# Second-table rows scaled in place by ScalarE and summed as accumulating transposes

## The chip, the cores and the metric

The kernel runs on one core of one Trainium2 chip. The metric is the device time of one execution in microseconds (us). Engine names in the profile: PE is TensorE, PEld its weight loads, DVE VectorE, ACT ScalarE, POOL GpSimd, SP SyncE.

## The reference

The input is 256 tokens of width 2048. A first block (two layers: sliding-window attention beside a gated recurrence, then stick-breaking attention) and a second block (a state-space group beside gated attention) come first; their matrix work fills about the first 1540 us. The change touches only what follows, a layer of looked-up experts ("peer"):

```
q = (t @ wq)...; s1, s2 = scores of q against two sets of 128 keys     # per token, 8 heads
idx, sc = top 16 of the sums of the top 16 of s1 and of s2             # 8 x 16 = 128 picks a token
g = softmax(sc)
act = gelu(einsum('thkd,td->thk', u[idx], t))                          # first table, rows of 2048 floats
out = einsum('thk,thkd->td', g * act, v[idx])                          # second table
x = x + out;  result = rmsnorm(x) * lnf_w
```

Both tables have 16384 rows of 2048 fp32. All arithmetic is fp32.

## The kernel before

**Picks.** Tokens lie on the 128 partitions, in two groups m = 0, 1. A "row" n of 256 is one pick for each of 128 tokens: n = 128 m + pick. For each row POOL starts one indirect DMA that fetches 128 rows of 8 KB (1 MB) of the first table into UROW (4 buffers) and one for the second table into VROW (5 buffers; the last four rows go into UROW). The last 16 blocks of 128 experts are "dense": they are not gathered (a pick that points there is skipped by the bounds check) but computed for all tokens, with table pieces that SP loads into DROW, 32 halves of 512 KB per table.

**First table.** DVE multiplies UROW with the tokens and sums along the row (L2162), one instruction a row. After every four rows ACT takes GELU (L1334), and DVE multiplies with the gates (`coefficients`, L2070), which gives COEF. DVE does this for batch q of four rows after its product of row 4q+5 and waits there for the GELU.

**Second table.** Row v runs V_LAG = 8 rows behind. In `diagonals` ACT makes a diagonal matrix of the 128 coefficients of a row (L1321, 128x128, four buffers). PE multiplies it with the row in four fp32 matmuls of 512 columns (`mm`, the last loop; the helper's line in the trace is L2223), accumulating in banks 0 to 3 with tokens on partitions. That completes row v and frees VROW (semaphore `v_used`). Every eighth row in two stretches, and four near the end, DVE adds itself in one instruction (`ON_DVE`, L2092). After row 127 DVE adds the banks to XR (`add_outputs`, at row 136), and PE waits for that before row 128.

**Order on the queues.** Every engine's order is written out by hand. POOL goes through n = 4 to 263: it waits until DVE is done with row n-4 and starts the fetch of row n of the first table (L668), then waits until VROW is free of row n-13 and starts the fetch of row n-8 of the second table (L676). ACT does, for each q: wait for four products, GELU of batch q, then `diagonals(q - 1)` with its other work for those rows beside it. PE takes the second-table rows in order, and beside them (`beside_row`) the dense work: for rows 2 to 109 turning pieces of the first table (L2785) and their products (`dense_dots`, 256 columns), for rows 112 to 158 gate matrices from one-hots, for rows 161 to 226 `dense_values`, the dense part of the second table, in which m = 1 goes to banks 0 to 3 (those of the rows) and m = 0 to banks 4 to 7. DVE adds banks 4 to 7 at row 236 (`add_dense`).

**The end.** DVE adds what is left, the squares, the root and the scaling follow, and SP stores the result.

Of the kernel before, what the change touches and what calls it, by code (L numbers as in the profile page):

```python
# [26 lines left out]
P = 128  # L27
# [23 lines left out]
HT_STEPS = 8  # L51
BATCH = 4
N_PICKS = MT * PICKS
ADD_AT = PICKS + 8
ADD_DENSE_AT, SUM_AT, SCALE_AT = PICKS + 108, PICKS + 113, PICKS + 121
ON_DVE = tuple(v for v in range(60, 108) if v % 8 == 7) + tuple(v for v in range(160, N_PICKS - 8) if v % 8 == 7)\
    + (N_PICKS - 7, N_PICKS - 5, N_PICKS - 4, N_PICKS - 2)
LATE = N_PICKS - 4
SHARED = N_PICKS - 1
LAST_ORDER = (2, 3, 0, 1)  # L60
# [28 lines left out]
def rows_before(rows, v):  # L89

    return sum(r < v for r in rows)
# [147 lines left out]
def two_blocks(nc, a, out):  # L239
    ctx = ExitStack()  # L240
    with ctx:
# [25 lines left out]
        with ExitStack() as rounded:  # L267
# [40 lines left out]

        names = """
            const_in ln_first vec_in masks vec_t cols_set x_in out_done eps_set act_chain dve_chain pool_chain  # L310
            w_full0 w_full1 w_full2 w_full3 w_gate0 w_gate1 w_gate2 w_gate3 g_t r_of r_v r_c r_hi r_lo r_one wh_done wl_done ws_used tile_free half_left low_out
            n_rstd n_root n_sq n_sum n_x n_t n_xt n_h n_l r_diag r_row r_set t_scaled y_ready y_h y_l
            aq_ready qk_t qk_c
            a_score a_soft a_exp a_rcp a_pn a_pt a_ptc a_pv
# [5 lines left out]
            k_in k_t k_c q_s q_sc tk_idx tk_e tk_g ln_in  # L320
            u_row0 u_row1 u_row2 u_row3 v_row0 v_row1 v_row2 v_row3 v_row4
            u_dot p_gelu p_coef p_diag v_used v_on o_add
            tt_set d_row0 d_row1 d_t d_tc d_m d_act d_v g_in g_g g_mix
            """.split()
        s = {n: sem(n) for n in names}
# [72 lines left out]
        GATE_PARTS = g_bf[:, 2048:2816].rearrange("p (k t) -> p k t", k=3)  # L398
        I1T, I2T, IOTA_B = g_bf[:, 2816:3072], g_bf[:, 3072:3328], g_bf[:, 3328:3456]
        G_REST = BIG[:, 13, 768:1024]  # L400
        DONE = [BIG[:, 12:14, :].rearrange("p a b -> p (a b)"), BIG[:, 10:12, :].rearrange("p a b -> p (a b)")]

        def v_buffer(v):
# [38 lines left out]
        @block.sync  # L442
        def _(sp):
            def load_tile(r, i, parity, first):
                t = r["base"] + i
                w = a[r["w"]]
                src = w.rearrange("(k p) n -> p k n", p=P)
                for j in range(4):
                    if r["base"] > 0 or not first:

                        sp.wait_ge(s["wl_done"], 8 * (t - 1) + (4 + j + 1 if HALVED[t - 1] else 2 * (j + 1)))
                    dst = RAW[:, j, :].rearrange("p (k n) -> p k n", k=4)[:, :, 0:r["width"]]
                    k0, col = 4 * j, i
                    if t == TWO_OUT - 1:
                        k0 = 4 * ((j + 2) % 4)
                    elif t in (TWO_OUT, TWO_OUT + 1):
                        k0, col = 4 * (j % 2) + (8 if t == TWO_OUT else 0), j // 2
                    c = bass.ds(r["c0"] + col * r["width"], r["width"])
                    if r["kind"] == "gate":

                        sp.dma_start(dst[:, :, 0:32], src[:, 4 * j:4 * j + 4, 2560:2592]).then_inc(s[f"w_gate{j}"], 16)
                        sp.dma_start(dst[:, :, 32:48], src[:, 4 * j:4 * j + 4, 5648:5664]).then_inc(s[f"w_full{j}"], 16)
                    else:
                        sp.dma_start(dst, src[:, k0:k0 + 4, c]).then_inc(s[f"w_full{j}"], 16)

            for m in range(MT):
                sp.dma_start(XR[:, m, :], a["x"][0].rearrange("(m p) d -> p m d", p=P)[:, m, :]).then_inc(s["x_in"], 16)
            for ph in PHASES:
                if ph == "peer_q":

                    sp.wait_ge(s["y_l"], 48)
                    keys = KEYS.rearrange("p (h f d) -> p h f d", h=PE_HEADS, f=2)
                    for f, name in enumerate(("peer_k1_2", "peer_k2_2")):
                        sp.dma_start(keys[:, :, f, :], a[name].rearrange("h n d -> n h d")).then_inc(s["k_in"], 16)
                over_tiles(sp, ph, load_tile)


            sp.wait_ge(s["k_t"], 4)
            sp.dma_start(LN2, a["ln2_w_2"].partition_broadcast(P)).then_inc(s["ln_in"], 16)
            def dense_half(name, k, b):  # L480

                r0, c0 = (KEPT + k // 2) * PE_KEYS, (k % 2) * (D // 2)
                sp.dma_start(DROW[:, b, :], a[name][r0:r0 + PE_KEYS, c0:c0 + D // 2]).then_inc(s[f"d_row{b}"], 16)

            sp.wait_ge(s["ws_used"], 8 * N_TILES)
            for k in range(2 * DENSE):
                if k >= 2:
                    sp.wait_ge(s["d_t"], HT_STEPS + 2 * (k - 1))
                dense_half("peer_u_2", k, k % 2)
            for k in range(2 * DENSE):  # L490
                if k < 2:
                    sp.wait_ge(s["d_t"], HT_STEPS + 2 * (2 * DENSE - 1 + k))
                else:
                    sp.wait_ge(s["d_v"], 2 * (k - 1))
                dense_half("peer_v_2", k, k % 2)
                if k == 4:
                    sp.wait_ge(s["u_dot"], PICKS)
                    sp.dma_start(LNF, a["lnf_w_2"].partition_broadcast(P)).then_inc(s["ln_in"], 16)

            rows = out[0].rearrange("(m p) d -> p m d", p=P)  # L500
            sp.wait_ge(s["n_x"], 2)
            sp.dma_start(rows[:, 0, :], DONE[0]).then_inc(s["out_done"], 16)
            for j in range(4):
                sp.wait_ge(s["n_x"], 3 + j)
                cs = slice(j * NW, (j + 1) * NW)
                sp.dma_start(rows[:, 1, cs], DONE[1][:, cs]).then_inc(s["out_done"], 16)
            sp.wait_ge(s["out_done"], 16 * 5)
# [210 lines left out]
        def _(act):  # L718
# [47 lines left out]
            def split(r, i, parity, first):  # L766
# [3 lines left out]
                for sub in range(8):  # L770
# [15 lines left out]
                    if sub % 2 == 0:  # L786
                        act.wait_ge(s[f"w_full{sub // 2}"], 16 * (t + 1))
                        if r["kind"] == "gate":
                            act.wait_ge(s[f"w_gate{sub // 2}"], 16)
                    if r["base"] > 0 or not first or sub >= 4:  # L790

                        act.wait_ge(s["ws_used"], 8 * t + (sub - 3))
# [509 lines left out]
            def beside_row(v):  # L1302
# [6 lines left out]
                if v == G_TURN_AT + 1:  # L1309
                    gates_turned()  # L1310

            def diagonals(q):

                act.wait_ge(s["p_coef"], q + 1)
                for n in range(BATCH * q, BATCH * (q + 1)):
                    if n not in ON_DVE:
                        k = rows_before(ON_PE, n)
                        if k >= 4:

                            act.wait_ge(s["v_used"], k - 3)  # L1320
                        act.activation(DIAG[:, k % 4, :], ID[:, :], ACT.Copy, scale=COEF[:, n:n + 1])\  # L1321
                            .then_inc(s["p_diag"], 1)
                    beside_row(n)

            gate_exp(0, 0, 1)
# [34 lines left out]
        def _(dve):  # L1360
# [708 lines left out]
                dve.wait_ge(s["p_gelu"], q + 1)  # L2069
                dve.tensor_tensor(COEF[:, cols], GELU[:, cols], KEPT_GATE[:, cols], ALU.mult).then_inc(s["p_coef"], 1)  # L2070

            def add_outputs():

                dve.wait_ge(s["v_used"], rows_before(ON_PE, PICKS))
                for j in range(4):
                    x = XR[:, 0, j * NW:(j + 1) * NW]
                    dve.tensor_tensor(x, x, bank[j], ALU.add).then_inc(s["o_add"], 1)

            def add_dense():

# [66 lines left out]
            for n in range(N_PICKS):  # L2147
# [28 lines left out]
                if n == GATES_AT:  # L2176
                    gates(1, 0, 4)
                    dve.sem_inc(s["g_in"], 1)
                if n == ADD_AT:
                    add_outputs()  # L2180
                if n == G_PARTS_AT:
                    gate_parts()
                for g in steps_at(MIX_AT, n):
# [22 lines left out]
            for at, j in enumerate(LAST_ORDER):  # L2206

                dve.wait_ge(s["v_used"], len(ON_PE) - (1 if at < 2 else 0))
                x = XR[:, 1, j * NW:(j + 1) * NW]
                dve.tensor_tensor(x, x, bank[j], ALU.add).then_inc(s["o_add"], 1)  # L2210
            root(1)

            dve.wait_ge(s["n_root"], 1)
# [7 lines left out]
        def _(pe):  # L2221
# [600 lines left out]
            def dense_values(i):  # L2822
# [4 lines left out]
                if c % 2 == 0:  # L2827
                    pe.wait_ge(s[f"d_row{c // 2}"], 16 * (DENSE + j + 1))
                cs = slice((c % 2) * NW, (c % 2 + 1) * NW)
                for m in range(MT):  # L2830
                    ins = mm(bank[4 * (1 - m) + c], ACTED[j // 8][:, j % 8, m * P:(m + 1) * P], DROW[:, c // 2, cs],
                             m == 0 and j == 0, m == 0 and j == DENSE - 1)
                ins.then_inc(s["d_v"], 1)

            def beside_row(v):

# [13 lines left out]
            for n in range(N_PICKS):  # L2850
# [2 lines left out]
                    continue  # L2853
                k = rows_before(ON_PE, n)
                m, pick = n // PICKS, n % PICKS
                if pick == 0 and m == 1:

                    pe.wait_ge(s["o_add"], 4)
                pe.wait_ge(s["p_diag"], k + 1)
                pe.wait_ge(s[v_landed(n)[0]], v_landed(n)[1])  # L2860
                for j in range(2 if n == SHARED else 4):
                    ins = mm(bank[j], DIAG[:, k % 4, :], v_buffer(n)[:, j * NW:(j + 1) * NW], pick == 0,
                             pick == PICKS - 1 or (n == SHARED - 1 and j >= 2))
                ins.then_inc(s["v_used"], 1)
                beside_row(n)


# [32 lines left out]
```

## Time and profile before

| | us |
|---|---|
| median of 2 runs (2814.39 and 2819.12) | 2816.76 |
| span of the profiled execution, first to last instruction | 2813.7 |
| median less span (the profiled execution has no time of its own beside its span) | 3.1 |
| PE busy | 2636.0 (94%) |
| DVE busy | 1755.5 (62%) |
| ACT busy | 1010.2 (36%) |
| POOL busy | 966.4 (34%) |

A busy share is an average over stages with different limits, so it doesn't say what bounds a stage. The column of DMA engines and the waits of a stage say more. On PE one fp32 matmul shows as two records. The page's 40 slices show two parts: up to about 1540 us the 16 DMA engines are 30% to 70% busy, after that 90% or more up to the end, at some 400 GB/s.

### The profile page before, as it was taken

To read this page: it belongs to the slowest core of one execution; us is meant where nothing else is said; L and a number is where in the kernel's file an instruction comes from. 1 tells how busy PE (TensorE), PEld (TensorE's weight loads), DVE (VectorE), ACT (ScalarE), POOL (GpSimd) and SP (SyncE) were. 2 spreads that over 40 slices of the span, in tenths; PEclk is the share of its full clock that TensorE was granted. 3 is DMA by queue.
4 is the path that set the end of the run, shared out by engine and by line. 5 is a ranking of instruction groups with operands and counts; after the bars stand their busy time and mean duration, and the time that the engine had idled before them with its cause. 6 is when DMAs were issued, how large, how long until landed. Compare 5 with 4: busy or idle time off the path is not lost.

```text
span 2813.7 us, 32400 instructions
## 1 busy us (share of the span) xinstructions
PE 2636.0 (94%) x12469; PEld 1852.2 (66%) x12469; DVE 1755.5 (62%) x2445; ACT 1010.2 (36%) x1667; POOL 966.4 (34%) x731
## 2 busy tenths in 40 slices
PE   8999999999999999999999799998988989899986
PEld 7877898888888888778789455555543434333432
DVE  4767564555456555567647787677657875455466
ACT  5567565544677454445553121111110000000011
POOL 6013151000000000441101654666556767355464
PEclk9999999999999999999999899999999999999998
DMA  7544403455445546434455999999999999999998
GB/s 239 183 145 146 144 16 136 163 205 188 156 141 177 175 133 215 145 120 150 135 180 196 368 404 404 410 405 411 413 407 391 396 398 410 416 398 412 414 410 328
DMA packets 209641, 751.53 MB, mean 267 GB/s; under 512 B 25133, under 2 KB 29449, under 8 KB 150857
## 3 DMA queue, kind: packets, MB, share of 16 engines
q0 software_dynamic: 74400, 475.38, 41.9%
q1 hardware_dynamic: 135088, 274.09, 28.4%
q8 instruction: 99, 1.62, 0.2%
q14 instruction: 54, 0.43, 0.0%
HBM read 809.09 MB, written 2.10 MB: 288 GB/s over the span
## 4 chain that ended last, share of the span: by engine, by line
DMA 25%; PE 24%; DVE 7%; POOL 5%; issue 5%; ACT 1%; POOLq 0%; DVEq 0%; ACTq 0%
PE bank L2223 24%; DMA UROW<-in_peer_u_dram,WORK 20%; DMA VROW<-in_peer_v_dram,WORK 5%; DVE BIG L2162 3%; POOL UROW L668 2%; POOL VROW L676 2%; DVE BIG L1721 0%; DVE WL L1421 0%; DMA UROW<-in_peer_v_dram,WORK 0%; DVE BIG L2117 0%; DVE UROW L2162 0%; PE bank L2359 0%; ACT WH L796 0%; PE bank L2785 0%; PE bank L2401 0%
## 5 line engine op out<-in xcount | busy, mean ns | idle before, releaser
L2223 PE MATMUL bank<-VROW,WORK 128*128 128x512 f32 x1864 | 863.6, 610 | 124.5 <-DMA VROW<-in_peer_v_dram,WORK 102.6
L2162 DVE CUSTOM_DVE_ANT_0 BIG<-UROW,BIG 128x2048 f32<-128x2048 f32 x252 | 578.3, 2295 | 398.9 <-DMA UROW<-in_peer_u_dram,WORK 383.6
L2223 PE MATMUL bank<-HX,WH 128*128 128x512 f32 (+1 forms) x2784 | 760.0, 345 | 12.0 <-issue 4.8
L2223 PEld LDWEIGHTS bank<-VROW,WORK 128*128 128x128 f32 x1864 | 353.1, 195 | 578.2 <-issue 534.8
L2223 PE MATMUL bank<-HX,WL 128*128 128x256 f32 x2128 | 596.7, 280 | 0.0
L2223 PEld LDWEIGHTS bank<-HX,WH 128*128 128x128 f32 x2784 | 480.5, 189 | 84.4 <-issue 16.9
L668 POOL DMA_INDIRECT UROW<-in_peer_u_dram,WORK x256 | 340.7, 1331 | 557.8 <-DVE WORK L2162 323.6
L1427 DVE TENSOR_TENSOR WL<-RAW,WH 128x1024 fp32r<-128x1024 f32 (+2 forms) x261 | 305.1, 1180 | 297.4 <-ACT WH L796 296.6
L2223 PE MATMUL bank<-WH,HX 128*128 128x512 f32 (+1 forms) x1472 | 452.1, 390 | 3.5 <-ACT BIG L739 2.5
L676 POOL DMA_INDIRECT VROW<-in_peer_v_dram,WORK x252 | 396.5, 1573 | 112.2 <-issue 76.3
L2223 PEld LDWEIGHTS bank<-HX,WL 128*128 128x128 f32 x2128 | 402.9, 189 | 0.1
L796 ACT ACTIVATE WH<-RAW 128x1024 fp32r<-128x1024 f32 (+2 forms) x261 | 261.5, 1019 | 217.0 <-PE bank L2223 212.9
L1421 DVE TENSOR_TENSOR WL<-RAW,WH 128x1024 fp32r<-128x1024 f32 x184 | 224.4, 1226 | 178.2 <-ACT WH L784 177.6
L2223 PEld LDWEIGHTS bank<-WH,HX 128*128 128x128 f32 x1472 | 270.9, 188 | 60.1 <-issue 4.5
L2223 PE MATMUL bank<-WL,HX 128*128 128x512 f32 (+1 forms) x736 | 284.2, 386 | 0.0
L784 ACT ACTIVATE WH<-RAW 128x1024 fp32r<-128x1024 f32 x184 | 191.6, 1056 | 146.5 <-PE bank L2223 130.7
L1334 ACT ACTIVATE WORK<-WORK 128x4 f32<-128x4 f32 x64 | 13.1, 204 | 625.4 <-DVE WORK L2162 625.3
L1284 ACT ACTIVATE BIG<-bank 128x512 f32<-128x512 f32 x64 | 38.2, 597 | 390.7 <-PE bank L2785 390.7
L623 POOL MEMSET AMB<- 128x256 f32 x1 | 0.3, 314 | 483.2 <-DVE HX L1801 483.2
L2223 PEld LDWEIGHTS bank<-WL,HX 128*128 128x128 f32 x736 | 138.7, 188 | 28.3
L630 POOL TENSOR_SCALAR ROWS<-ROWS,AMB 128x256 fp32r<-128x256 f32 x32 | 43.6, 1364 | 268.0 <-DVE ROWS L1710 220.0
L2223 PE MATMUL bank<-HT,BIG 128*128 128x256 f32 x512 | 121.1, 380 | 0.0
(386 smaller groups left out, 2393.3 us busy)
## 6 DMA issues: line engine op xcount, KB each, us to landing
RAW<-in_w_in_odd_dram SPq DMA_DIRECT2D x64, 1024.0 KB, 5.4
RAW<-in_w_in_even_dram SPq DMA_DIRECT2D x48, 1024.0 KB, 5.2
RAW<-in_w_in_dram SPq DMA_DIRECT2D x44, 1024.0 KB, 5.1
RAW<-in_w_out_even_dram SPq DMA_DIRECT2D x16, 1024.0 KB, 5.0
RAW<-in_w_out_odd_dram SPq DMA_DIRECT2D x16, 1024.0 KB, 5.1
RAW<-in_w_out_dram SPq DMA_DIRECT2D x16, 1024.0 KB, 5.2
RAW<-in_peer_wq_dram SPq DMA_DIRECT2D x16, 1024.0 KB, 5.1
DROW<-in_peer_u_dram SPq DMA_DIRECT2D x32, 512.0 KB, 7.8
```

Of the source, the lines that this page charges most:

```text
L623: link(pool.memset(AMB[:, 0:256], 0.0))
L630: return pool.tensor_scalar(ROW_HEAD[h % 2], ROW_ALL.bitcast(F32), ROW_OF[:, h:h + 1], None, ALU.mult)\
L668: pool.indirect_dma_start(UROW[:, n % ROWS_EACH, :], None, a["peer_u_2"], bass.IndirectOffsetOnAxis(ap=PICK[:, n // PICKS, n % PICKS:n % P ...
L676: pool.indirect_dma_start(v_buffer(v), None, a["peer_v_2"], bass.IndirectOffsetOnAxis(ap=PICK[:, v // PICKS, v % PICKS:v % PICKS + 1], axi ...
L784: act.activation(halves(WH, sub), raw_half(sub), ACT.Copy).then_inc(s["wh_done"], 1)
L796: act.activation(WH[:, sl:sl + 2, 0:w], raw[:, k0:k0 + 2, 0:w], ACT.Copy)\
L1284: act.activation(UT[:, i % 2, :], bank[4 + i % 2], ACT.Copy).then_inc(s["d_tc"], 1)
L1334: act.activation(GELU[:, cols], DOT[:, cols], ACT.Gelu).then_inc(s["p_gelu"], 1)
L1421: dve.tensor_tensor(halves(WL, sub), raw_half(sub), halves(WH, sub).bitcast(F32), ALU.subtract)\
L1427: dve.tensor_tensor(WL[:, sl:sl + 2, 0:w], raw[:, k0:k0 + 2, 0:w], WH[:, sl:sl + 2, 0:w].bitcast(F32), ALU.subtract).then_inc(s["wl_done"], 1)
L2162: dve.tensor_tensor_reduce(out=product, in0=UROW[:, b, :], in1=TT[m], op0=ALU.mult, op1=ALU.add, scale=1.0, scalar=0.0, accum_out=DOT[:, n ...
L2223: return pe.matmul(dst, lhsT, rhs, start=start, stop=stop, skip_group_check=True)
```

## The change

- ACT no longer makes diagonals for rows below `TURNED` = 244. It waits for the row itself and multiplies it in place by its coefficients (`Copy` with a scale per partition, 128x2048). PE then turns the row in 16 fp32 transposes of 128x128 against the identity, which accumulate in banks 0 to 3: the sums stand there turned, model dimension on partitions.
- The last 12 rows go on as before, into banks 4 to 7.
- After row 127 and after row 243 ACT copies banks 0 to 3 to a work tile (`sums_out`, four copies of 128x512), and PE turns them back (`turn_back`, four groups of four transposes): for m = 0 into banks 4 and 5 in turn, after rows 128, 130, 132 and 134, from where DVE adds them at rows 139, 141, 143 and 145; for m = 1 into banks 4 to 7 right after row 244.
- `dense_values` computes m = 1 turned as well: four matmuls of 128 columns, with the table piece as weights, in place of one of 512.
- Row 247 moves from DVE to PE. The load of the last norm's weights by SP waits for another semaphore. Two gate semaphores are merged into two others.

```diff
-ADD_AT = PICKS + 8
+ADD_AT = PICKS + 11
-ON_DVE = ... tuple(v for v in range(160, N_PICKS - 8) if v % 8 == 7)
+ON_DVE = ... tuple(v for v in range(160, N_PICKS - 12) if v % 8 == 7)
+TURNED = N_PICKS - 12
+BACK_AT = tuple(PICKS + 2 * g for g in range(4))
...
-                    sp.wait_ge(s["u_dot"], PICKS)
+                    sp.wait_ge(s["o_add"], 4)
...
+            def sums_out(m):
+                act.wait_ge(s["v_used"], rows_before(ON_PE, TURNED if m else PICKS))
+                if m:
+                    act.wait_ge(s["d_v"], V_STEPS)
+                for j in range(4):
+                    act.activation(WIDE[m][:, j * NW:(j + 1) * NW], bank[j], ACT.Copy).then_inc(s["w_out"], 1)
...
                 for n in range(BATCH * q, BATCH * (q + 1)):
-                    if n not in ON_DVE:
+                    if n == PICKS:
+                        sums_out(0)
+                    if n < TURNED and n not in ON_DVE:
+                        act.wait_ge(s[v_landed(n)[0]], v_landed(n)[1])
+                        act.activation(v_buffer(n), v_buffer(n), ACT.Copy, scale=COEF[:, n:n + 1])\
+                            .then_inc(s["p_diag"], 1)
+                    elif n not in ON_DVE:
...
+                    if n == TURNED:
+                        sums_out(1)
...
-            def add_outputs():
-                dve.wait_ge(s["v_used"], rows_before(ON_PE, PICKS))
-                for j in range(4):
-                    x = XR[:, 0, j * NW:(j + 1) * NW]
-                    dve.tensor_tensor(x, x, bank[j], ALU.add).then_inc(s["o_add"], 1)
+            def add_outputs(j):
+                dve.wait_ge(s["w_t"], j + 1)
+                x = XR[:, 0, j * NW:(j + 1) * NW]
+                dve.tensor_tensor(x, x, bank[4 + j % 2], ALU.add).then_inc(s["o_add"], 1)
...
-                for m in range(MT):
-                    ins = mm(bank[4 * (1 - m) + c], ACTED[j // 8][:, j % 8, m * P:(m + 1) * P], DROW[:, c // 2, cs],
-                             m == 0 and j == 0, m == 0 and j == DENSE - 1)
+                mm(bank[4 + c], ACTED[j // 8][:, j % 8, 0:P], DROW[:, c // 2, cs], j == 0, j == DENSE - 1)
+                for q in range(4):
+                    ins = mm(bank[c][:, q * P:(q + 1) * P], DROW[:, c // 2, (c % 2) * NW + q * P:(c % 2) * NW + (q + 1) * P],
+                             ACTED[j // 8][:, j % 8, P:T], False, False)
...
+            def turn_back(m, g):
+                pe.wait_ge(s["w_out"], 4 * m + g + 1)
+                if m == 0 and g >= 2:
+                    pe.wait_ge(s["o_add"], g - 1)
+                for q in range(4):
+                    c0 = g * NW + q * P
+                    ins = pe.matmul(bank[4 + (g if m else g % 2)][:, q * P:(q + 1) * P], WIDE[m][:, c0:c0 + P], ID[:, :],
+                                    start=m == 0 and q == 0, stop=False, is_transpose=True, skip_group_check=True)
+                ins.then_inc(s["w_t"], 1)
...
-                if pick == 0 and m == 1:
-                    pe.wait_ge(s["o_add"], 4)
+                if n == PICKS:
+                    pe.wait_ge(s["w_out"], 4)
+                if n == TURNED:
+                    pe.wait_ge(s["o_add"], 8)
                 pe.wait_ge(s["p_diag"], k + 1)
-                pe.wait_ge(s[v_landed(n)[0]], v_landed(n)[1])
-                for j in range(2 if n == SHARED else 4):
-                    ins = mm(bank[j], DIAG[:, k % 4, :], v_buffer(n)[:, j * NW:(j + 1) * NW], pick == 0, ...)
+                if n < TURNED:
+                    for c in range(KT):
+                        ins = pe.matmul(bank[c // 4][:, c % 4 * P:(c % 4 + 1) * P], v_buffer(n)[:, c * P:(c + 1) * P], ID[:, :],
+                                        start=pick == 0 and c % 4 == 0, stop=False, is_transpose=True, skip_group_check=True)
+                else:
+                    pe.wait_ge(s[v_landed(n)[0]], v_landed(n)[1])
+                    for j in range(2 if n == SHARED else 4):
+                        ins = mm(bank[4 + j], DIAG[:, k % 4, :], v_buffer(n)[:, j * NW:(j + 1) * NW], n == TURNED, ...)
                 ins.then_inc(s["v_used"], 1)
+                if n in BACK_AT:
+                    turn_back(0, BACK_AT.index(n))
+                if n == TURNED:
+                    for g in range(4):
+                        turn_back(1, g)
```

## Rows read from the trace of the kernel before

**Rows 1.** Windows, four stages: us, busy of PE PEld DVE ACT POOL, clock, DMA share, GB/s.

```profile
1574.00:2124.00 550.00, 518.67 (x1622) 284.97 (x1621) 399.13 (x721) 91.52 (x229) 313.96 (x224) 0.98 1.01 407
2124.00:2360.00 236.00, 207.26 (x1182) 96.44 (x1181) 183.24 (x231) 18.29 (x62) 174.70 (x101) 0.99 0.98 395
2360.00:2744.00 384.00, 350.39 (x787) 149.04 (x785) 198.42 (x184) 30.24 (x97) 199.86 (x154) 0.98 1.01 411
2744.00:2800.00 56.00, 39.34 (x78) 16.02 (x78) 34.00 (x29) 5.31 (x16) 29.08 (x19) 0.90 0.96 387
```

**Rows 2.** Lines, 1700 to 2150 us: busy, mean ns | idle before, releasers.

```profile
L2223 PE MATMUL bank<-VROW,WORK 128*128 128x512 f32 x681 | 313.8, 608 | 33.0 <-DMA VROW<-in_peer_v_dram,WORK 32.7
L2162 DVE CUSTOM_DVE_ANT_0 BIG<-UROW,BIG 128x2048 f32<-128x2048 f32 x91 | 208.8, 2294 | 127.0 <-DMA UROW<-in_peer_u_dram,WORK 116.4 <-issue 7.1 <-DVE WORK L1747 3.0
...
L1321 ACT ACTIVATE WORK<-ID,WORK 128x128 f32<-128x128 f32 x86 | 30.9, 391 | 5.2 <-PE bank L2223 5.2
```

**Rows 3.** Lines, 2360 to 2744 us.

```profile
L2223 PE MATMUL bank<-VROW,WORK 128*128 128x512 f32 x536 | 249.1, 609 | 33.6 <-DMA VROW<-in_peer_v_dram,WORK 33.3
L2162 DVE CUSTOM_DVE_ANT_0 BIG<-UROW,BIG 128x2048 f32<-128x2048 f32 x76 | 174.6, 2298 | 186.0 <-DMA UROW<-in_peer_u_dram,WORK 185.9
L2223 PE MATMUL bank<-DROW,BIG 128*128 128x512 f32 x251 | 116.7, 593 | 0.0
...
L668 POOL DMA_INDIRECT UROW<-in_peer_u_dram,WORK x77 | 89.3, 1160 | 157.8 <-DVE WORK L2162 133.8 <-PE bank L2223 14.2 <-issue 9.8
```

**Rows 4.** Lines, 2124 to 2360 us.

```profile
L668 POOL DMA_INDIRECT UROW<-in_peer_u_dram,WORK x51 | 97.9, 1919 | 48.2 <-DVE WORK L2162 30.4 <-issue 11.3 <-PE bank L2223 6.6
```

**Rows 5.** Page, DMA issues: count, median us from issue to landing.

```profile
UROW<-in_peer_u_dram,WORK POOLq DMA_INDIRECT x256, 15.8
VROW<-in_peer_v_dram,WORK POOLq DMA_INDIRECT x252, 17.0
```

**Rows 6.** Waits, 1800 to 2700 us: total us, times, longest us.

```profile
DVE BIG L2162 <- DMA UROW<-in_peer_u_dram,WORK: 313.6, 139, 5.2
...
PE bank L2223 <- DMA VROW<-in_peer_v_dram,WORK: 77.0, 61, 4.3
...
POOL UROW L668 <- PE bank L2223: 38.2, 14, 6.3
```

**Rows 7.** Timeline of PE from 1850 us: start, us, instructions.

```profile
1850.27 3.60 PE L2223 MATMUL bank<-VROW,WORK 128*128 128x512 f32 x8
1853.71 0.60 PE L2785 MATMUL bank<-ID,DROW 128*128 128x128 f32 x4
1854.14 1.89 PE L2223 MATMUL bank<-HT,BIG 128*128 128x256 f32 x8
1855.87 6.49 PE L2223 MATMUL bank<-VROW,WORK 128*128 128x512 f32 x14
```

**Rows 8.** Lines of ACT, 0 to 1500 us: two widths with a scale per partition.

```profile
L908 ACT ACTIVATE WORK<-WORK,SM 128x128 f32<-128x128 f32 x32 | 12.9, 403 | 88.2 <-DVE SM L1590 61.3 <-DVE SM L1587 26.9
...
L937 ACT ACTIVATE WORK<-WORK,SM 128x384 f32<-128x384 f32 x16 | 9.9, 617 | 0.2
```

**Rows 9.** Timeline of PE around the transposes at 1549 us.

```profile
1544.75 2.02 PE L2223 MATMUL bank<-BIG 128*128 128x128 f32 x16 [1.27 <-ACT BIG L752]
1549.29 5.38 PE L2774 MATMUL bank<-ID,BIG 128*128 128x128 f32 x32 [2.51 <-DVE BIG L2154]
```

**Rows 10.** Windows within those transposes, columns as in the first group.

```profile
1550.00:1551.00 1.00, 1.00 (x6) 1.00 (x5) 0.00 (x0) 0.55 (x1) 0.70 (x2) 0.50 1.08 336
...
1553.00:1554.00 1.00, 1.00 (x12) 1.00 (x11) 0.00 (x0) 1.00 (x3) 0.98 (x1) 1.00 0.96 328
```

**Rows 11.** Windows: the fastest 25 us of the gathers.

```profile
2750.00:2775.00 25.00, 21.15 (x44) 8.46 (x43) 15.88 (x15) 1.08 (x4) 14.57 (x11) 0.91 1.01 422
```

**Rows 12.** Timeline near the end.

```profile
2749.34 13.31 PE L2223 MATMUL bank<-VROW,WORK 128*128 128x512 f32 x24 [5.08 <-DMA VROW<-in_peer_v_dram,WORK]
...
2778.04 1.07 POOL L676 DMA_INDIRECT VROW<-in_peer_v_dram,WORK  x1 [3.90 <-PE bank L2223]
```

More of the change, by code:

```diff
@@ L53 @@
 N_PICKS = MT * PICKS
-ADD_AT = PICKS + 8
+ADD_AT = PICKS + 11
 ADD_DENSE_AT, SUM_AT, SCALE_AT = PICKS + 108, PICKS + 113, PICKS + 121
-ON_DVE = tuple(v for v in range(60, 108) if v % 8 == 7) + tuple(v for v in range(160, N_PICKS - 8) if v % 8 == 7)\
+ON_DVE = tuple(v for v in range(60, 108) if v % 8 == 7) + tuple(v for v in range(160, N_PICKS - 12) if v % 8 == 7)\
     + (N_PICKS - 7, N_PICKS - 5, N_PICKS - 4, N_PICKS - 2)
+TURNED = N_PICKS - 12
+BACK_AT = tuple(PICKS + 2 * g for g in range(4))
 LATE = N_PICKS - 4
@@ L310, in two_blocks @@
             const_in ln_first vec_in masks vec_t cols_set x_in out_done eps_set act_chain dve_chain pool_chain
-            w_full0 w_full1 w_full2 w_full3 w_gate0 w_gate1 w_gate2 w_gate3 g_t r_of r_v r_c r_hi r_lo r_one wh_done wl_done ws_used tile_free half_left low_out
+            w_full0 w_full1 w_full2 w_full3 w_gate0 w_gate1 g_t r_of r_v r_c r_hi r_lo r_one wh_done wl_done ws_used tile_free half_left low_out
             n_rstd n_root n_sq n_sum n_x n_t n_xt n_h n_l r_diag r_row r_set t_scaled y_ready y_h y_l
@@ L322, in two_blocks @@
             u_dot p_gelu p_coef p_diag v_used v_on o_add
+            w_out w_t
             tt_set d_row0 d_row1 d_t d_tc d_m d_act d_v g_in g_g g_mix
@@ L400, in two_blocks @@
         G_REST = BIG[:, 13, 768:1024]
+        WIDE = [BIG[:, 0:2, :].rearrange("p a b -> p (a b)"), BIG[:, 10:12, :].rearrange("p a b -> p (a b)")]
         DONE = [BIG[:, 12:14, :].rearrange("p a b -> p (a b)"), BIG[:, 10:12, :].rearrange("p a b -> p (a b)")]
@@ L459, in load_tile @@
                     if r["kind"] == "gate":
-                        sp.dma_start(dst[:, :, 0:32], src[:, 4 * j:4 * j + 4, 2560:2592]).then_inc(s[f"w_gate{j}"], 16)
+                        sp.dma_start(dst[:, :, 0:32], src[:, 4 * j:4 * j + 4, 2560:2592]).then_inc(s[f"w_gate{j // 2}"], 16)
                         sp.dma_start(dst[:, :, 32:48], src[:, 4 * j:4 * j + 4, 5648:5664]).then_inc(s[f"w_full{j}"], 16)
@@ L788, in split @@
                         if r["kind"] == "gate":
-                            act.wait_ge(s[f"w_gate{sub // 2}"], 16)
+                            act.wait_ge(s[f"w_gate{sub // 4}"], 32)
                     if r["base"] > 0 or not first or sub >= 4:
@@ L1315, in diagonals @@
                 for n in range(BATCH * q, BATCH * (q + 1)):
-                    if n not in ON_DVE:
+                    if n == PICKS:
[5 more added lines that the diff above has]
+                    elif n not in ON_DVE:
                         k = rows_before(ON_PE, n)
-                        if k >= 4:
+                        if n >= TURNED + 4:
                             act.wait_ge(s["v_used"], k - 3)
@@ L2178, in _ @@
                     dve.sem_inc(s["g_in"], 1)
-                if n == ADD_AT:
-                    add_outputs()
+                j = step_at(n, ADD_AT, 2, 4)
+                if j is not None:
+                    add_outputs(j)
                 if n == G_PARTS_AT:
@@ L2209, in _ @@
                 x = XR[:, 1, j * NW:(j + 1) * NW]
-                dve.tensor_tensor(x, x, bank[j], ALU.add).then_inc(s["o_add"], 1)
+                dve.tensor_tensor(x, x, bank[4 + j], ALU.add).then_inc(s["o_add"], 1)
             root(1)
@@ L2855, in _ @@
                 m, pick = n // PICKS, n % PICKS
-                if pick == 0 and m == 1:
-                    pe.wait_ge(s["o_add"], 4)
+                if n == PICKS:
+                    pe.wait_ge(s["w_out"], 4)
+                if n == TURNED:
+                    pe.wait_ge(s["o_add"], 8)
                 pe.wait_ge(s["p_diag"], k + 1)
-                pe.wait_ge(s[v_landed(n)[0]], v_landed(n)[1])
-                for j in range(2 if n == SHARED else 4):
-                    ins = mm(bank[j], DIAG[:, k % 4, :], v_buffer(n)[:, j * NW:(j + 1) * NW], pick == 0,
-                             pick == PICKS - 1 or (n == SHARED - 1 and j >= 2))
-                ins.then_inc(s["v_used"], 1)
+                if n < TURNED:
[5 more added lines that the diff above has]
+                    for j in range(2 if n == SHARED else 4):
+                        ins = mm(bank[4 + j], DIAG[:, k % 4, :], v_buffer(n)[:, j * NW:(j + 1) * NW], n == TURNED,
+                                 n == (SHARED if j < 2 else SHARED - 1))
+                ins.then_inc(s["v_used"], 1)
+                if n in BACK_AT:
[3 more added lines that the diff above has]
+                        turn_back(1, g)
                 beside_row(n)
```

## The prediction

> **What bounds the kernel now.** The change acts only after 1540 us, so I cut the rest into stages: windows first, for what is full in each; then lines, for what each engine's idle time ended on; then waits and timeline, for the price of one step. In the windows [rows 1] the DMA column is the one to read. While pieces of the first table's dense part run (1574 to 2124 us) and while those of the second run (2360 to 2744), the 16 DMA engines are busy for a share of 1.01, at 407 and 411 GB/s. PE is nearly full too, 518.67 of 550 us and 350.39 of 384, so which of the two ends last has to be seen in the waits. DVE's idle time before its product ends on a landing of the first table: 116.4 of 127.0 us in one stage, 185.9 of 186.0 in the other; PE waits for landings of the second table, 32.7 and 33.3 us [rows 2, 3]. In the other direction POOL waited for PE to free a buffer for 38.2 us in 900, against 313.6 us of DVE waiting for DMA [rows 6].
>
> The buffers say the same. 91 products in 450 us [rows 2] are one pair (a row of each table) per 4.95 us. A fetch takes 15.8 or 17.0 us from issue to landing [rows 5], so 3.2 of 4 and 3.4 of 5 buffers are always in flight. Those times are queueing: at 407 GB/s a pair with its dense piece is 2.0 MB in 4.95 us. DMA is the bound, PE is a close second, and the change moves no byte.
>
> **The change part by part.**
>
> *Rows on PE.* A row starts every 3.44 us (1850.27 to 1853.71), a dense turn of four transposes takes 0.43, its eight product records 1.73 [rows 7]. 16 transposes at 0.43/4 are 1.72 us, so a row saves 1.72. That is 85 rows (681 records by 8) or 146 us of PE in 450 [rows 2], and 67 rows or 115 us in 384 [rows 3]. Transposes that accumulate are not in the trace: below, the plain transpose; above, two records of an fp32 matmul of 128 columns at 2.02/16 = 0.126 [rows 9], which makes 4.0 us a row. I take 1.72, the same instruction. At 4.0, with 0.93 rows and 0.6 dense steps a pair (64 over 107 rows), PE needs 5.0 against 4.95 us in the first stage and about 5.1 against 5.05 in the third: some +12 us in all. This is one bound.
>
> *Rows on ACT.* Two widths give 0.836 ns an element ((617-403)/256) [rows 8], and 128x2048 comes to 403 + 1920 x 0.836 = 2.0 us. Bounds: 1.6 (fixed part hidden) and 3.7 (six pieces of 384). I take 2.0, since the fixed part stands in both rows. ACT spends 91.5 us of 550 now [rows 1], 0.82 a pair; less the diagonal (30.9 us for 91 pairs, 0.34 [rows 2]) plus 2.0 it is 2.5 of 4.95 us, at 3.7 it is 4.2. ACT has room, and this work lies beside the fetches.
>
> *How long a buffer is held.* Landing to release was 3.6 us (one row on PE) and becomes 2.0 + 1.72 + some 0.3 for the handover, 4.0. The cycle, 17.0 + 4.0 = 21.0 us, must be under five spacings, 24.75. It is, so the wait added on ACT delays no fetch. With that cover gone (over 7.75 us held) the excess would be paid in every row.
>
> *What is queued behind ACT's new wait.* GELU of batch q stands behind the scaling of row 4q-5, whose fetch POOL issues right behind first-table row 4q+3, on the same queue. It lands half a spacing later (2.5 us), then 2.0 for the scaling and 0.2 for GELU. DVE asks for it after its product of row 4q+5, which is two spacings and 2.3 us [rows 2] after row 4q+3 landed, 12.2. Slack 7.5 us: nothing.
>
> *Dense values.* 63 steps (251 records by 4) of 1.72 us [rows 3] become 0.86 + 8 x 0.126 [rows 9] = 1.87: +9 us of PE, taken from the 115 saved. PE falls to about 3.1 of 5.05 us a pair there and to 2.9 in the first stage (1.72 x 0.93 + 0.6 x 2.16).
>
> *Turning back.* For m = 0 four copies of some 0.72 us (403 + 384 x 0.836) on ACT [rows 8], 2.9 us, then 16 transposes; row 128 is released about 5 us late, once, with 3.4 rows in flight to cover it. In exchange DVE no longer waits at row 136 for row 127. Nothing, up to +5 uncovered. For m = 1 the same stands in front of row 245, while rows 236 to 243 leave PE earlier. Today POOL waits there for PE (3.90 us at 2778.04 [rows 12]) before its last fetches. I set -3 to +3, and take 0. Row 247 off DVE: DVE waits for landings there, 0. The semaphore changes on SP and ACT lie behind work that is long done: 0.
>
> *What comes late next.* DMA stays. What is won is only DMA time lost to late releases. If all four stages ran at the 411 GB/s of the third, the first would take 5.4 us less, the second 9.2, the last 3.3 [rows 1]. In the second POOL needs 1919 ns to issue a first-table fetch against 1160 later [rows 3, 4] and DVE is busy for 183 of 236 us; neither is touched. I take 3 us in the first stage and 2 in the second. The profiled span is 2813.7, the median lies 3.1 above: 2813.7 - 5 + 3.1 = about 2812.
>
> **The rivals.**
>
> *PE's clock falls* (slower). PE will idle for 40% of these stages. For it: after a pause of 5.08 us, 24 records took 13.31 us, 0.55 each in place of 0.43 [rows 12]. At 1.2 GHz throughout, row and steps double (3.44, 4.32, 3.74): 5.79 us a pair in the first stage against 4.95, over 111 pairs +93; 6.13 against 5.05 in the third, over 76 pairs +82; together about 2987. It decides only when the clock is low for over some 65% to 70% of a stage; below that PE still keeps up. Against it: at 1549.29 us 32 transposes ran alone on PE after 2.51 us of idling [rows 9]; they began at a clock of 0.50, six records per us, and within 4 us it was 1.00, twelve per us [rows 10]. So transposes alone brought the clock up. 5%.
>
> The Trainium skill says the opposite (TensorE: Matmul & The Clock Gate, Part 4: PE-mode transpose): a transpose does not count as busy for the clock. By that rule the sum would be this rival's 2987; the rows just named disagree with it.
>
> *ACT and DVE take turns* (slower). If second-table rows land later than the queue order suggests, GELU comes late, DVE stops, and first-table fetches with it: a scaling of 2.0 us exposed in each of 61 batches is +122, about 2937. It decides when the 7.5 us of slack is gone. Against it: both tables' fetches share one queue and land within 17 us. 5%.
>
> *DMA was held back by PE* (faster). If it could hold the best 25 us, 422 GB/s [rows 11], the 496.6 MB of the four stages (rate times length [rows 1]) would take 1177 us in place of 1226: -49, about 2768. Against it: the share reads 1.01 in that slice and in whole stages alike. Even this stays within 2%. 4%, of which 3% beyond.
>
> The Trainium skill has a ceiling above that rate (DMA: Bandwidth & Descriptors, Where 436 GB/s comes from): 435 GB/s. By it, an estimate, these stages would take 1142 us and the kernel about 2732; no row shows that rate.
>
> *The transposes take as long as the matmuls did* (the change doesn't shorten PE). Then DMA hides them anyway: up to the +12 above, about 2829. It lies inside the forecast.
>
> **How the numbers follow.** Forecast, DMA-bound as before: 86%, 2812. The low end is half-way from 411 to 422 GB/s in every stage: 1192 us, -34, so 2784. The high end adds the bounds +12, +5 and +3 to a zero gain: 2837. What is left out is the two slow rivals and a little on each side. 2% is 56 us, about what a measurement of this kernel tells from no change. Faster 3%, slower 9% (a slow rival at part of its price may stay inside), within 88%.
>
> **What would show it.** Right: DMA share still 1.00 or more with 405 to 415 GB/s in the same stages, PE busy at 55% to 65%, one ACT instruction of 2.0 us a row, 16 records a row about 0.11 apart, DVE idle on first-table landings as before. Wrong: a granted clock near 0.5 over whole stages, DVE waiting for ACT (L2070) in every batch, POOL waiting for second-table buffers, or a DMA share under 0.95. What I trust least is the order of landings behind ACT's new wait.

## The result and the profile after

The changed kernel takes 2838.41 us (2838.04 and 2838.79), against 2816.76 before: ratio 1.0083, 95% interval 1.0063 to 1.0102. It is slower by 22 us, 0.8%, and its time lies just above the range that was given. The profiled span is 2836.3 us, 22.6 more than before.

Windows of the changed kernel over the same four stages as [rows 1], same columns:

```profile
1574.00:2124.00 550.00, 386.01 (x2432) 347.68 (x2432) 393.14 (x713) 259.07 (x224) 301.41 (x221) 0.88 1.00 401
2124.00:2360.00 236.00, 153.33 (x1590) 141.87 (x1590) 182.92 (x234) 104.75 (x71) 172.26 (x100) 0.80 0.97 390
2360.00:2744.00 384.00, 271.62 (x1699) 225.01 (x1700) 192.12 (x178) 135.57 (x87) 191.73 (x149) 0.89 1.01 409
2744.00:2800.00 56.00, 30.05 (x153) 25.44 (x152) 33.66 (x32) 24.04 (x30) 36.66 (x22) 0.73 0.86 341
```

PE was relieved (518.67 us of 550 became 386.01, 350.39 of 384 became 271.62) and its granted clock fell. The gathers got nothing from it: 401, 390 and 409 GB/s stand where 407, 395 and 411 stood, and 341 where 387 stood. So the question is where DMA went idle. Two stretches of the first and the last stage hold most of it; first the kernel before, then the changed one:

```profile
1635.00:1735.00 100.00, 96.89 (x305) 52.51 (x304) 83.43 (x192) 23.52 (x49) 52.33 (x40) 1.00 1.00 402
2725.00:2775.00 50.00, 39.30 (x83) 15.68 (x82) 30.10 (x28) 7.88 (x18) 36.23 (x22) 0.93 1.01 420
```

```profile
1635.00:1735.00 100.00, 74.05 (x464) 67.44 (x463) 80.54 (x181) 53.72 (x49) 52.64 (x37) 0.88 0.96 379
2725.00:2775.00 50.00, 21.91 (x125) 20.16 (x126) 27.71 (x24) 23.34 (x23) 31.34 (x19) 0.72 0.82 323
```

The bytes that were not moved there, at 410 GB/s, are worth (402 - 379) x 100 / 410 = 5.6 us and (420 - 323) x 50 / 410 = 11.8 us, together 17 of 22. In both, DVE stood still and waited for ACT. Its waits for ACT (changed kernel, 1574 to 2800 us: total us, times, longest us):

```profile
DVE SM L2081 <- ACT WORK L1262: 15.7, 3, 7.1
DVE SM L2156 <- ACT BIG L1265: 13.6, 1, 13.6
DVE BIG L2119 <- ACT BIG L1304: 3.0, 1, 3.0
```

The kernel before, same view and stretch, has 6.7 us of them in place of 32.3, and none for the squares:

```profile
DVE SM L2060 <- ACT WORK L1258: 6.0, 3, 2.6
...
DVE BIG L2099 <- ACT BIG L1300: 0.7, 1, 0.7
```

The first is the sum of the gates (the softmax over a token's picks) after rows 22, 30 and 38, which needs an exponential of ACT (`gate_exp`); the second the sum of four squares of ACT, for the last norm, after row 241; the third the parts of the turned gates at row 119. The second of them in the timeline of ACT, DVE and POOL:

```profile
2741.39 2.00 ACT L1333 ACTIVATE VROW<-VROW,WORK 128x2048 f32<-128x2048 f32 x1 [2.44 <-DMA VROW<-in_peer_v_dram,WORK]
2743.30 0.61 ACT L1265 ACTIVATE BIG<-XR 128x512 f32<-128x512 f32 x1
...
2746.30 0.16 DVE L2156 TENSOR_REDUCE SM<-SM 128x1 f32<-128x4 f32 x1 [13.63 <-ACT BIG L1265]
...
2749.51 2.50 POOL L672 DMA_INDIRECT UROW<-in_peer_u_dram,WORK  x1 [13.48 <-DVE WORK L2182]
```

The squares need nothing that a landing brings. But in ACT's order they stand behind the scaling of rows 232 to 235, and the last of these began only when its row had landed, at 2741.39. DVE stood for 13.63 us, its products stopped, and POOL, which starts a first-table fetch only after a product and a second-table fetch only after that one, issued no fetch for 13.48 us.

### The profile page after: what moved, and what is told of

Read it like the earlier page. It is cut to its first block, busy times and chain, and to the rows that moved or that the text cites. A ratio compares the mean times of both kernels' runs of the same rounds, so it can differ in the third digit from the quotient of the medians.

```text
span 2836.3 us, 36680 instructions
## 1 busy us (share of the span) xinstructions
PE 2376.3 (84%) x14717; PEld 2050.3 (72%) x14717; DVE 1751.9 (62%) x2444; ACT 1390.7 (49%) x1676; POOL 960.5 (34%) x731
## 4 chain that ended last, share of the span: by engine, by line
DMA 27%; PE 22%; DVE 8%; issue 5%; POOL 4%; ACT 2%; POOLq 0%; DVEq 0%; ACTq 0%
DMA UROW<-in_peer_u_dram,WORK 19%; PE bank L2244 19%; DMA VROW<-in_peer_v_dram,WORK 7%; DVE BIG L2182 4%; POOL UROW L672 2%; POOL VROW L680 2%; PE bank L2899 2%; ACT VROW L1333 1%; DVE BIG L1742 0%; DVE WL L1442 0%; DMA UROW<-in_peer_v_dram,WORK 0%; DVE UROW L2182 0%; PE bank L2380 0%; ACT WH L800 0%; DVE WORK L1765 0%
## 5 line engine op out<-in xcount | busy, mean ns | idle before, releaser
L2899 PE MATMUL bank<-ID,VROW 128*128 128x128 f32 x3648 | 549.4, 315 | 404.8 <-ACT VROW L1333 404.4
L2899 PEld LDWEIGHTS bank<-ID,VROW 128*128 128x128 f32 x3648 | 491.8, 163 | 456.5 <-ACT VROW L1333 449.5
L1333 ACT ACTIVATE VROW<-VROW,WORK 128x2048 f32<-128x2048 f32 x228 | 455.9, 2001 | 613.6 <-DMA VROW<-in_peer_v_dram,WORK 613.6
L672 POOL DMA_INDIRECT UROW<-in_peer_u_dram,WORK x256 | 359.6, 1405 | 599.2 <-DVE WORK L2182 364.1
L680 POOL DMA_INDIRECT VROW<-in_peer_v_dram,WORK x252 | 371.9, 1476 | 99.9 <-issue 79.0
L2244 PE MATMUL bank<-BIG 128*128 128x16 bf16 (+4 forms) x1240 | 102.6, 223 | 7.2 <-POOL BIG L613 2.3
```

The source lines that it names most:

```text
L672: pool.indirect_dma_start(UROW[:, n % ROWS_EACH, :], None, a["peer_u_2"], bass.IndirectOffsetOnAxis(ap=PICK[:, n // PICKS, n % PICKS:n % P ...
L680: pool.indirect_dma_start(v_buffer(v), None, a["peer_v_2"], bass.IndirectOffsetOnAxis(ap=PICK[:, v // PICKS, v % PICKS:v % PICKS + 1], axi ...
L1333: act.activation(v_buffer(n), v_buffer(n), ACT.Copy, scale=COEF[:, n:n + 1])\
L2244: return pe.matmul(dst, lhsT, rhs, start=start, stop=stop, skip_group_check=True)
L2899: ins = pe.matmul(bank[c // 4][:, c % 4 * P:(c % 4 + 1) * P], v_buffer(n)[:, c * P:(c + 1) * P], ID[:, :], start=pick == 0 and c % 4 == 0, ...
```

## The experiments

Ratios are to runs of the kernel before beside them on the same chip, with 95% intervals; its medians there were 2814.93 (first four), 2815.42 (next four) and 2815.39 us.

**e1, squares first.**

```diff
+                if q == ADD_DENSE_AT // BATCH:
+                    act.wait_ge(s["o_add"], 8)
+                    for b in range(4):
+                        square(b, b)
+                if q == SUM_AT // BATCH:
+                    root(0)
                 if q >= 1:
                     diagonals(q - 1)
-                if q == ADD_DENSE_AT // BATCH: ...
```

> ScalarE's four squares and its root for m = 0 stand ahead of the scaling of rows 232 to 239 instead of behind it. Theory (VectorE waits for work of ScalarE that stands behind a wait for a landing): the 13.6 us wait of VectorE at row 241 goes, and with it the 11 us that the gathers lose between 2735 and 2785 us; about 2827 us. Rival 1 (TensorE's lower clock makes each row hold its buffer longer): no change, 2838. Rival 2 (ScalarE's 2.0 us a row itself is the loss): no change, 2838.

Measured 2826.99 us, 1.0039 (1.0026 to 1.0053), 11 less than the changed kernel. DVE's wait is gone and the second stretch is full again:

```profile
2734.25 0.15 DVE L2156 TENSOR_REDUCE SM<-SM 128x1 f32<-128x4 f32 x1
```

```profile
1635.00:1735.00 100.00, 72.21 (x453) 65.50 (x452) 79.19 (x180) 54.48 (x49) 51.21 (x36) 0.88 0.96 375
2725.00:2775.00 50.00, 24.78 (x145) 22.04 (x144) 33.23 (x32) 26.57 (x26) 42.84 (x23) 0.76 1.01 415
```

**e2, gates first.**

```diff
-                if q in (5, 7, 9):
-                    gate_exp(0, (q - 3) // 2, 1)
...
                 act.activation(GELU[:, cols], DOT[:, cols], ACT.Gelu).then_inc(s["p_gelu"], 1)
...
+                if q in (4, 6, 8):
+                    gate_exp(0, (q - 2) // 2, 1)
                 if q >= 1:
                     diagonals(q - 1)
```

> ScalarE's three exponentials of the gates (for rows 22, 30 and 38) stand one batch earlier, ahead of the scaling of four rows. Theory: VectorE's three waits of together 15.7 us go, and the gathers get back the 5 to 6 us they lose up to 1735 us; about 2833 us. Rivals 1 and 2: no change, 2838.

Measured 2831.16 us, 1.0054 (1.0040 to 1.0068): 7 less. Here it is the first stretch that is full:

```profile
1635.00:1735.00 100.00, 74.16 (x463) 66.86 (x462) 83.44 (x190) 54.34 (x47) 49.48 (x40) 0.89 1.01 403
2725.00:2775.00 50.00, 23.22 (x141) 21.12 (x140) 25.63 (x24) 24.32 (x24) 30.57 (x21) 0.74 0.83 322
```

**e3, both.** The two edits together.

> Both moves. Theory: the gains add, some 17 us; about 2821 us, with 4 to 5 us above the kernel before left for the stage of the gate matrices. Rivals 1 and 2: 2838, no change.

Measured 2820.39 us, 1.0015 (1.0006 to 1.0024): 18 of the 22 us are back, the sum of the single gains. Both stretches read as in the kernel before, at a clock of 0.89 and 0.70:

```profile
1635.00:1735.00 100.00, 73.93 (x463) 66.86 (x462) 83.52 (x191) 54.36 (x47) 49.08 (x40) 0.89 1.00 403
2725.00:2775.00 50.00, 29.65 (x160) 26.44 (x158) 30.50 (x30) 24.66 (x19) 40.83 (x24) 0.70 1.01 418
```

**e4, clock up.** The changed kernel, with

```diff
+                    if n == 0:
+                        act.activation(DIAG[:, 3, :], ID[:, :], ACT.Copy, scale=0.0)
...
+                if 4 <= n < 244:
+                    for i in range(3):
+                        mm(bank[i][:, 0:T], DIAG[:, 3, :], HT[:, n % KT, :], False, False)
                 pe.wait_ge(s["p_diag"], k + 1)
```

> The changed kernel with three extra matmuls of 256 columns with zero weights ahead of rows 4 to 243 on TensorE (about 1.3 us a row at full clock), which add zero to the sums and keep TensorE busy. Theory: the granted clock comes up to about 0.98 in the gathers and the time stays at 2838 within 3 us, since a row's buffer is free in time at either clock. Rival 1 (clock): 8 to 22 us faster, 2816 to 2830. Rival 2: no change.

Measured 2837.28 us, 1.0078 (1.0064 to 1.0092): unchanged, while the clock did come up. Its windows over the first three stages:

```profile
1574.00:2124.00 550.00, 476.65 (x3048) 427.97 (x3049) 392.71 (x713) 258.92 (x223) 302.03 (x222) 0.97 1.00 401
2124.00:2360.00 236.00, 188.58 (x1899) 164.51 (x1898) 184.55 (x234) 104.21 (x70) 172.30 (x99) 0.99 0.98 392
2360.00:2744.00 384.00, 335.56 (x2089) 278.82 (x2089) 190.01 (x178) 136.21 (x89) 192.23 (x148) 0.95 1.00 407
```

0.97, 0.99 and 0.95 in place of 0.88, 0.80 and 0.89, at the same rates. The clock cost nothing here. The extra matmuls load PE themselves, by some 1.3 us a row, so this run alone could hide a gain of that size; but slow rows would delay fetches in the main by way of second-table buffers that are freed late, and POOL's waits for those are 9.1 us here and 9.8 in the changed kernel (1574 to 2800 us), too little to hide much.

**e5, the wait alone.** The kernel before, with

```diff
+                        act.wait_ge(s[v_landed(n)[0]], v_landed(n)[1])
                         act.activation(DIAG[:, k % 4, :], ID[:, :], ACT.Copy, scale=COEF[:, n:n + 1])\
```

> The kernel before, with one addition: ScalarE waits for the row to land before it makes the row's diagonal. No transposes, no scaling. Theory (the loss is VectorE waiting for work that ScalarE holds behind landings): most of the 22 us comes with this wait alone, less 1.7 us for each wait since a diagonal takes 0.3 us and a scaling 2.0: some 4 us up to 1735 us and 9 at the end, about 2828 us (2824 to 2832). Rival (the transposes, the scaling or the clock cost the time): 2815, no change.

Measured 2832.32 us, 1.0063 (1.0050 to 1.0077): 17 us, just over the top of the band and more than the 13 that were expected. One wait in ACT's queue, with no transpose and no scaling in the kernel, brings three quarters of the loss, and the same three waits of DVE (same view):

```profile
DVE SM L2061 <- ACT WORK L1258: 13.4, 3, 6.0
DVE SM L2137 <- ACT BIG L1261: 12.1, 1, 12.1
DVE BIG L2100 <- ACT BIG L1300: 1.5, 1, 1.5
```

**e6, half the rows' matmuls.** The kernel before, with

```diff
-                for j in range(2 if n == SHARED else 4):
+                for j in range(2 if n == SHARED else 2 if 8 <= pick < 120 else 4):
```

> The kernel before, with half of the row's product left out on TensorE for picks 8 to 119 (columns 1024 to 2047 of these rows are not added): 3.44 us of TensorE a row become 1.72, nothing else changes. Theory (DMA bounds the gathers, a faster TensorE is worth a few us at most): 2810 to 2815. Rival (TensorE bounded them and the change lost the gain elsewhere): 2795 or less.

The run leaves out half of the columns of rows 8 to 119 of each group. Measured 2814.62 us, 0.9994 (0.9985 to 1.0003). PE was relieved of as much as by the change (403.68 of 550 us busy, 265.48 of 384), and it was worth nothing:

```profile
1574.00:2124.00 550.00, 403.68 (x1232) 224.46 (x1231) 401.70 (x724) 91.77 (x229) 303.99 (x224) 0.89 1.01 408
2124.00:2360.00 236.00, 175.50 (x1047) 78.24 (x1046) 180.78 (x229) 18.99 (x64) 177.89 (x103) 0.85 0.98 395
2360.00:2744.00 384.00, 265.48 (x512) 103.33 (x510) 199.03 (x185) 30.58 (x99) 198.11 (x153) 0.89 1.01 412
```

**e7, turned gates too.** Both moves, and

```diff
+                    if n == G_TURN_AT + 1:
+                        gates_turned()
                     if n < TURNED and n not in ON_DVE:
```

with the call taken out of the work beside the row.

> Both moves, and ScalarE's three copies of the turned gates ahead of the scaling of row 111 in place of behind it. Theory: the last wait of VectorE for ScalarE behind a landing (3.0 us at row 119) goes; 1 to 3 us faster than with both moves, about 2818. Rivals: 2820, no change.

Measured 2818.97 us, 1.0011 (1.0002 to 1.0020). The time fits, but it doesn't stand clear of e3's, and the reason given was a miss: DVE still waits 2.58 us. The copies no longer wait for row 111 to land, they wait for PE, which turns the gates after row 110, and that row is scaled only after its own landing. PE's and ACT's timeline:

```profile
2115.24 3.58 PE L2897 MATMUL bank<-ID,VROW 128*128 128x128 f32 x16 [2.09 <-ACT VROW L1332]
...
2119.57 0.38 ACT L1302 ACTIVATE BIG<-bank 128x256 bf16<-128x256 f32 x1 [4.39 <-PE bank L2827]
```

**e8, both moves and the clock.** The edits of e3 and e4.

> Both moves and the extra matmuls with zero weights that keep TensorE's clock up. What is left with both moves is some 5 us, 4 of them between 2110 and 2360 us. Theory: the clock has no part in it, 2820 within 2 us. Rival (rows that take 3.0 to 3.7 us at the lower clock make it): 4 to 5 us faster, about 2816.

Measured 2821.10 us, 1.0019 (1.0010 to 1.0029): no gain over e3. What is left after the moves isn't the clock either.

**e9, rows off DVE.** The three moves, and

```diff
-ON_DVE = tuple(... range(60, 108) ...) + tuple(... range(160, N_PICKS - 12) ...) + (N_PICKS - 7, ...)
+ON_DVE = (N_PICKS - 7, N_PICKS - 5, N_PICKS - 4, N_PICKS - 2)
```

> All three moves (squares, gates, turned gates), and the rows that VectorE added itself before row 244 go to ScalarE and TensorE like the others: VectorE loses 16 instructions of 2.35 us. Theory (DMA bounds, and VectorE's idle time ends on landings): no change from the three moves alone, 2817 to 2821. Rival (VectorE's load is what still holds back first-table fetches): 3 to 8 us faster, which would be under the kernel before.

Measured 2818.72 us, 1.0013 (1.0004 to 1.0022): no change, so DVE's own load wasn't what held fetches back.

**e10, scaled twice.** The three moves, and a second `Copy` with scale 1.0 over every scaled row.

> All three moves, and every scaled row is passed through ScalarE a second time with a scale of 1.0: 2.0 us more of ScalarE a row, and a buffer held 2.0 us longer (some 6 us at full clock, up to 8 at the lower one, against 7.75 at which the prediction said that it decides). Theory (only the order of ScalarE's work cost time, its length is covered): at most 5 us slower than 2819, 2819 to 2824. Rival 2 (ScalarE's time a row is a cost): some 10 us or more slower, 2829 and up.

Measured 2824.94 us, 1.0034 (1.0022 to 1.0046), 6 us more than e7: a little over the band, and below the rival's 10 and more. The length of ACT's work isn't quite free, but it is cheap. ACT's busy time in the first stage rose from 261.58 to 457.25 us. POOL's wait for second-table buffers, in e7 and in e10 (1800 to 2700 us):

```profile
POOL VROW L680 <- PE bank L2897: 0.6, 2, 0.3
```

```profile
POOL VROW L680 <- PE bank L2899: 71.1, 48, 5.2
```

With 2.0 us more the buffers came late in 48 rows. Worked out row by row for the same stretch from the landings and PE's timeline, a row was held for 4.3 us in e7 and 6.5 here (medians), and from issue to release it took longer than the prediction's limit of 24.75 us in 13 of 166 rows there and in 53 of 165 here: the limit stands where the prediction had put it. Over 1574 to 2800 us the waits are 106.7 us in 70 rows, against 5.0 in three in e7, and even so the price was only 6 us. A part of them took the place of another wait: POOL's waits ahead of first-table fetches fell from 421 to 300 us.

No version beat the kernel before: with e6 showing that a relieved PE is worth nothing there, the best of the moved versions are still 1.0011 and 1.0013 of it, both intervals above 1. The stages from 2124 to 2744 us hold these last 3 us (390 and 409 GB/s in e7 against 395 and 411 [rows 1]), and neither the clock (e8) nor DVE's load (e9) accounts for them. But some 2 of them can be placed: they stand at the start of the stage from 2124 us, and not in the rest of it. The kernel before, then e7:

```profile
2115.00:2165.00 50.00, 42.16 (x235) 19.70 (x234) 40.96 (x54) 5.25 (x18) 33.76 (x21) 1.00 0.95 381
2165.00:2360.00 195.00, 172.21 (x969) 79.96 (x968) 149.30 (x187) 15.32 (x52) 144.24 (x85) 0.99 0.99 399
```

```profile
2115.00:2165.00 50.00, 31.56 (x315) 29.69 (x316) 41.11 (x54) 21.31 (x17) 33.95 (x20) 0.81 0.90 362
2165.00:2360.00 195.00, 133.62 (x1332) 123.40 (x1331) 147.37 (x186) 87.10 (x56) 146.44 (x85) 0.78 1.00 399
```

That is (381 - 362) x 50 / 410 = 2.3 us. In this stretch DVE waits for the turned gates and works on them between two products, and POOL pauses ahead of a first-table fetch, for 8.10 us in e7 against 6.26 before (the kernel before, then e7; the PE that the first line names is no cause, since a first-table fetch waits for DVE's product alone):

```profile
2127.83 2.51 POOL L668 DMA_INDIRECT UROW<-in_peer_u_dram,WORK  x1 [6.26 <-PE bank L2223]
```

```profile
2129.14 2.51 POOL L672 DMA_INDIRECT UROW<-in_peer_u_dram,WORK  x1 [8.10 <-DVE WORK L2180]
```

So the third of DVE's waits, which the move of e7 didn't take away, is the likely cause. No run without it was made: this is argued and not shown, and the rest is open.

## Why the prediction was wrong

**The bound: right.** DMA bound the gathers; halving PE's row work changed the time by a ratio of 0.9994 (e6). The 5 us that I took as won did not show (at most 4 by the interval), nor did the 18 us of a rate of 411 throughout. One reading under it was wrong: the 38.2 us of [rows 6] are not waits for PE. A first-table fetch waits for DVE's product alone, and all 14 of these started 0.8 to 1.1 us after the product's signal, as the others did; PE's signal for the second-table fetch behind it came in between, and the view names the later one. What POOL did wait for PE stands at the second-table fetches; the kernel before, then e6 (1800 to 2700 us):

```profile
POOL VROW L676 <- PE bank L2223: 10.9, 9, 1.7
```

```profile
POOL VROW L676 <- PE bank L2223: 1.3, 2, 1.0
```

So there were 11 us of late releases in 900, and taking them away won nothing that could be measured.

**The single prices: right.** One scaling is 2001 ns (estimate 2.0 us), and 16 transposes are 1.97 us to the end of the last at full clock (1.72 from start to start was taken). A row in PE's timeline of the changed kernel, and its lines, 1700 to 2150 us:

```profile
1701.35 1.97 PE L2899 MATMUL bank<-ID,VROW 128*128 128x128 f32 x16 [0.82 <-ACT VROW L1333]
```

```profile
L2899 PE MATMUL bank<-ID,VROW 128*128 128x128 f32 x1332 | 194.3, 308 | 138.4 <-ACT VROW L1333 138.2
...
L1333 ACT ACTIVATE VROW<-VROW,WORK 128x2048 f32<-128x2048 f32 x84 | 168.1, 2001 | 217.6 <-DMA VROW<-in_peer_v_dram,WORK 217.6
```

PE's idle time now ends on ACT, ACT's on landings. The hold of a buffer, put at 4.0 us against a limit of 7.75, measured 4.15 in the median (1800 to 2700 us, landing to the end of the last transpose), and the limit stood the test of e10. Two sums are off by a little, and nothing rests on them: from 2812 the rival of ACT and DVE comes to 2934, not 2937, and the low end of the range to 2783, not 2784.

**The step that failed: "What is queued behind ACT's new wait".** It followed GELU alone and found 7.5 us of slack, which held: GELU is not among DVE's three waits. But ACT's queue carries three other pieces on which DVE waits, and all stood behind landings now: e5, the new wait alone, cost 17 us, and e3, which takes the gates and the squares out from behind it, got 18 back. By its heading the step had to name all that is queued, and it stopped at the piece that comes every four rows; the four squares and the root were passed over in "Turning back", the gates named nowhere. Their price could be worked out, all but the length of the squares from the rows: row 235 is fetched after DVE's product of row 239, lands 17.0 us later [rows 5], takes 2.0 of scaling and 3.0 of squares (2743.30 to 2746.30 in the timeline above), and DVE is ready for the sum two spacings after that product, 9.9 us. That makes 12.1 us before POOL's issue time is added; 13.63 was measured. For the gates of row 22, which stood behind row 15, it is 17.0 + 2.0 less three spacings, 14.9: 4.1 us before the issue, the exponential and its table load (1.3 us, L1262); 7.1 was the longest.

That 2838 lies so near the top of the range is chance: the 20 us there were bounds of other terms, slower transposes and an uncovered turning back, which cost nothing here.

**Turning back and row 247: right** as terms of zero, as far as the rates tell; no run tests them singly. For m = 0 the four copies took 2.07 us (2.9 estimated), and 2165 to 2360 us, where it is turned back, ran at 399 GB/s in e7 as before. With the waits moved, e3 ran the last gathers at 418 GB/s.

**The rivals.** *PE's clock falls*: it did, to 0.88, 0.80 and 0.89. Between the levels of 1.0 and 0.5 that is 24%, 40% and 22% of a stage at the low one, well short of the two thirds from which it would decide, and e4 shows that it cost nothing. *ACT and DVE take turns* had the right pair of engines and the wrong place: not every batch, 122 us, but five waits of 32 us together; the four that e3 moved away were worth 18 us of time. *DMA was held back by PE*: refuted by e6.

**The rule on transposes.** The changed kernel has PE busy for 386.01 of 550 us at a clock of 0.88, mostly with transposes (241.1 us of the rows, 44.7 of the dense pieces); e6 has it busy for 403.68, mostly with matmuls, at 0.89. In the third stage it is 271.62 of 384 (154.1 of them transposes) at 0.89, and 265.48 at 0.89. The Trainium skill has it that transposes don't count as busy for the clock in the same way (TensorE: Matmul & The Clock Gate, Part 4: PE-mode transpose). These runs don't bear that out for fp32 transposes: at the same busy share the clock came out alike.

## What to carry to other kernels

Where a wait for a transfer is added to an engine's queue, list everything that stands behind it in that queue for the next few batches, the rare pieces first, and ask of each who waits for it; work that doesn't need the transfer belongs ahead of the wait. Here one line of waiting, with no other work, brought 17 of 22 us (e5), and moving two short pieces ahead of it brought 18 back (e3). And relieving an engine that is 90% busy beside full DMA queues may be worth nothing: leaving out half of its work on the rows says so in one run (e6).

## What the hardware showed unexpectedly

Matmuls with all-zero weights held the granted clock up as others do: 0.97 against 0.88 in the first stage (e4). And small delays of single fetches cost little while others are in flight: 106.7 us of waits for second-table buffers, spread over 70 rows and in part in place of other waits, cost 6 us (e10), while a single pause of 13.5 us, with no fetch of either table issued, cost 11 (e1).
